# An in-place block solve in two half-groups, work moved between three engines, and adjacent parts for the feed-forward input

## The reference, cut to what matters

```
def _rwkv7_step(S, inp):
    r, w, k, v, a, b = inp
    sa = jnp.einsum('bhvk,bhk->bhv', S, a)
    S = S * w[:, :, None, :] + sa[..., None] * b[:, :, None, :] + v[..., None] * k[:, :, None, :]
    y = jnp.einsum('bhvk,bhk->bhv', S, r)
    return S, y
...
    mean = jnp.mean(y, axis=-1, keepdims=True)
    var = jnp.mean(jnp.square(y - mean), axis=-1, keepdims=True)
    yn = ((y - mean) * lax.rsqrt(var + LNX_EPS)).reshape(B, T, D) * lnx_w + lnx_b
    bonus = (jnp.sum(rh * kh * r_k, axis=-1, keepdims=True) * vh).reshape(B, T, D)
    out = ((yn + bonus) * g).astype(x.dtype)
    return out @ w_o
...
def conv_ffn(x, w_in, conv_w, conv_b, w_out):
    gate, up = jnp.split(x @ w_in, 2, axis=-1)
```

## Time and profile before

| | |
|---|---|
| median of 3 runs | 1096.93 us |
| profiled execution | 1099.76 us, span 1097.9 us |
| TensorE busy | 1071.0 us (98%) |
| VectorE busy | 801.8 us (73%) |
| ScalarE busy | 605.1 us (55%) |
| GpSimd busy | 209.3 us (19%) |
| granted TensorE clock, mean | 0.997 of full speed |
| L288, x960 | 339.8 us busy, 399 ns each |
| L289, x960 | 269.6 us busy, 281 ns each |

### The profile page before, as it was taken

One profiled execution on the slowest core, in us unless ns is written; L12 is line 12 of the kernel. 1 busy time (PEld: TensorE's weight loads), 2 busy tenths in 40 slices (PEclk: granted clock), 3 DMA queues, 4 the chain that ended last, 5 costly groups with the idle time before them and its releaser, 6 DMA issues.

```text
span 1097.9 us, 19100 instructions
## 1 busy us (share of the span) xinstructions
PE 1071.0 (98%) x7335; PEld 924.8 (84%) x7335; DVE 801.8 (73%) x1134; ACT 605.1 (55%) x928; POOL 209.3 (19%) x230
## 2 busy tenths in 40 slices
PE   7999989999999999999999999999999999999997
PEld 6997788888888889789888888998777789888886
DVE  7997887778885758777788746688867776655543
ACT  6765354556664566856566544635665445545532
POOL 0134552112221011001222200470100001122200
PEclk9999999999999999999999999999999999999999
DMA  8553181646666566345667575456452654666552
GB/s 250 170 170 115 46 262 43 172 116 192 185 189 228 196 148 161 118 130 146 188 188 194 174 286 158 155 192 213 148 140 83 194 166 131 184 189 191 192 191 77
DMA packets 219748, 183.13 MB, mean 167 GB/s; under 512 B 43265, under 2 KB 197614, under 8 KB 219678
## 3 DMA queue, kind: packets, MB, share of 16 engines
q1 hardware_dynamic: 215710, 171.43, 52.1%
q0 software_dynamic: 3392, 8.66, 2.5%
q10 hardware_dynamic: 576, 2.07, 0.5%
HBM read 179.44 MB, written 2.69 MB: 166 GB/s over the span
## 4 chain that ended last, share of the span: by engine, by line
PE 82%; DVE 12%; issue 2%; ACT 1%; POOL 1%; DMA 1%; SPq 0%; DVEq 0%; POOLq 0%; ACTq 0%
PE bank L288 21%; PE bank L282 13%; PE bank L284 13%; PE bank L283 13%; PE bank L289 10%; PE bank L295 3%; DVE ring L413 3%; PE bank L1238 2%; DVE arena L1655 1%; DVE arena L1750 1%; DVE stat L1748 1%; PE bank L371 1%; PE bank L2123 1%; PE bank L1353 1%; DVE arena L1680 0%
## 5 line engine op out<-in xcount | busy, mean ns | idle before, releaser
L413 DVE TENSOR_TENSOR ring<-ring,arena 128x2048 fp32r<-128x2048 f32 (+1 forms) x138 | 312.3, 2266 | 113.0 <-ACT arena L407 111.4
L282 PE MATMUL bank<-arena 128*128 128x512 f32 (+3 forms) x980 | 343.8, 351 | 2.0 <-DVE ring L413 1.6
L288 PE MATMUL bank<-arena 128*128 128x512 f32 x960 | 339.8, 399 | 0.0
L407 ACT ACTIVATE arena<-ring 128x2048 fp32r<-128x2048 f32 (+1 forms) x145 | 272.0, 1879 | 93.0 <-DMA ring<-in_ffn_w_out 43.2
L289 PE MATMUL bank<-arena,ring 128*128 128x256 f32 x960 | 269.6, 281 | 0.0
L284 PE MATMUL bank<-arena 128*128 128x512 f32 (+3 forms) x720 | 264.9, 368 | 0.0
L288 PEld LDWEIGHTS bank<-arena 128*128 128x128 f32 x960 | 180.4, 188 | 44.7
L283 PE MATMUL bank<-ring,arena 128*128 128x512 f32 (+2 forms) x560 | 216.2, 386 | 0.0
L282 PEld LDWEIGHTS bank<-arena 128*128 128x128 f32 x980 | 185.5, 189 | 27.1 <-issue 3.7
L289 PEld LDWEIGHTS bank<-arena,ring 128*128 128x128 f32 x960 | 181.5, 189 | 0.0
L284 PEld LDWEIGHTS bank<-arena 128*128 128x128 f32 x720 | 135.6, 188 | 22.3
(11 more groups left out here) (335 smaller groups left out, 1282.7 us busy)
## 6 DMA issues: line engine op xcount, KB each, us to landing
ring<-in_ffn_w_in SPq DMA_DIRECT2D x80, 512.0 KB, 5.1
ring<-in_ffn_w_out SPq DMA_DIRECT2D x44, 512.0 KB, 4.4
ring<-in_w_gate_up SPq DMA_DIRECT2D x40, 512.0 KB, 5.1
ring<-in_w_in SPq DMA_DIRECT2D x18, 1024.0 KB, 5.0
ring<-in_a_w_rkv SPq DMA_DIRECT2D x12, 1024.0 KB, 5.5
ring<-in_w_down SPq DMA_DIRECT2D x22, 512.0 KB, 3.7
ring<-in_a_w_o SPq DMA_DIRECT2D x4, 1024.0 KB, 8.4
arena<-in_ffn_w_in SPq DMA_DIRECT2D x8, 512.0 KB, 4.7
```

The source lines that it names most:

```text
L282: nc.tensor.matmul(dst, stationary[0], moving[0], start=start, stop=False)
L288: nc.tensor.matmul(dst[:, :], stationary[0], both_parts, start=start, stop=False)
L407: nc.scalar.activation(buf(hi_of(n), 0, w, arena12), ring[:, r, 0:w], ACT.Copy).then_inc(hi_ready, 1)
L413: on.tensor_tensor(ring12[:, r, 0:w], ring[:, r, 0:w], buf(hi_of(n), 0, w, arena12).bitcast(F32), ALU.subtract).then_inc(split_ready, 1)
```

## The change

The solve goes by blocks and in place. `block_sweep(a, parts)` computes one block of 32 rows for one half of the heads (g = 0 or 1, 8 heads): 8 matmuls with a stationary operand of 32 columns. Where two parts are given, the two are different row blocks of the two halves, and their matmuls alternate. `block_added` adds those 32 rows (32 x 512) into the right side itself. Half 1 runs one stage behind half 0. `block_inverses` is the old last sweep, one half at a time. `steps` leaves out the first 32 columns. Centring goes from 16 ScalarE instructions a chunk to one on GpSimd, into a buffer of its own; the bonus product goes from VectorE to 16 ScalarE instructions a chunk, and its addition of the shift to GpSimd. SyncE's order changes around w_o, `load_z` and `early_in`. The two parts of the feed-forward input lie next to each other for each chunk of 128 channels, so the 512 columns are one piece.

```diff
-            i, j = sorted((i, j))
-            return arena12[0][:, i:j + 1:j - i, :].rearrange("p s (c t) -> p s c t", t=T)
+            return bufs(i, 2, arena12).rearrange("p (c x t) -> p c x t", x=2, t=T)
...
-        FFN_H, FFN_H_LO, FFN_F, FFN_F_LO, FFN_CONV, FFN_P = (12, 0, 0), (10, 5, 5), 1, 6, 4, 9
+        FFN_H, FFN_F, FFN_F_LO, FFN_CONV, FFN_P = (11, 10, 11), 1, 6, 4, 9
...
-            h2, h_parts = chan2(FFN_H[f], FFN_H_LO[f]), beside(FFN_H[f], FFN_H_LO[f])
+            h2 = parts_of(FFN_H[f])
+            h_parts = bufs(FFN_H[f], 2, arena12).rearrange("p (c n) -> p c n", n=2 * T)
...
-                    mm = nc.tensor.matmul(bank[4 + b % 4][:, i * P:(i + 1) * P], z[a][:, h, :], n_off[a][:, h, :],
+                    mm = nc.tensor.matmul(bank[4 + b % 4][:, i * P + BS:(i + 1) * P], z[a][:, h, :], n_off[a][:, h, BS:P],
...
+            def block_sweep(a, parts):
+                for g, b in parts:
+                    if b > 1:
+                        pe.wait_ge(sum_ready, SUM_NO[a][g, b - 1])
+                    elif a == 0:
                         pe.wait_ge(u_rhs, g + 1)
+                        pe.wait_ge(step_in, 2 * (g + 1))
                     else:
+                        pe.wait_ge(sum_ready, STATE_ADDED + g + 1)
+                        pe.wait_ge(step_in, STEP_BANKS)
+                for i in range(8):
+                    for g, b in parts:
+                        h, cells = 8 * g + i, rows_of_block(b)
+                        mm = nc.tensor.matmul(bank[g][cells, i * N:(i + 1) * N], n_off[a][:, h, cells],
+                                              rhs[a][:, h * N:(h + 1) * N], start=True, stop=True)
+                        if i == 7:
+                            mm.then_inc(sweep_mm, 1)
...
+            def bonus_scaled(a, half):
+                for h in range(8 * half, 8 * half + 8):
+                    op = nc.scalar.activation(bonus[a][:, h // 2, h % 2 * N:(h % 2 + 1) * N], toks(W_V)[:, a, h * N:(h + 1) * N],
+                                              ACT.Copy, scale=bon[:, a * H + h:a * H + h + 1])
...
+            def block_added(a, g, b):
+                rows, cells = rows_of_block(b), slice(g * HALF, (g + 1) * HALF)
+                dve.wait_ge(sweep_mm, SOLVED * a + SWEEP_NO[g, b])
+                nc.vector.tensor_tensor(rhs[a][rows, cells], bank[g][rows, :], rhs[a][rows, cells], ALU.add).then_inc(sum_ready, 1)
...
+            def values_centred(a):
+                pool.wait_ge(means_ready, a + 1)
+                pool.wait_ge(u_mm, 2 * (a + 1))
...
+            def rest_gated(a):
...
+                pool.wait_ge(bonus_copied, NT + a + 1)
+                nc.gpsimd.tensor_tensor(rest[a], bonus[a], chunks(buf(W_LNX, D, 2 * D)), ALU.add).then_inc(c_ready, 1)
+                pool.wait_ge(c_ready, 3 * a + 1)
+                nc.gpsimd.tensor_tensor(rest[a], rest[a], chunks(g), ALU.mult).then_inc(c_ready, 1)
+                pool.wait_ge(c_ready, 3 * a + 2)
                 nc.gpsimd.tensor_tensor(g, g, buf(W_LNX, 0, D), ALU.mult).then_inc(c_ready, 1)
...
+            values_centred(0)
+            values_centred(1)
+            pool.wait_ge(lnx_landed, 32)
+            rest_gated(0)
+            rstd(0)
+            rstd(1)
+            rest_gated(1)
+            rstd(2)
+            rstd(3)
...
+            rows_of("w_o", A["a_w_o"][0], 2, range(0, 1))
             rwkv_inverse_late_sp(sp, 0)
-            rows_of("w_o", A["a_w_o"][0], 2, range(0, 2))
+            rows_of("w_o", A["a_w_o"][0], 2, range(1, 2))
             rwkv_inverse_late_sp(sp, 1)
             rows_of("w_o", A["a_w_o"][0], 2, range(2, 4))
-            sp.wait_ge(sweep_mm, sweeps_before(0, SWEEPS + 1) + 2)
+            sp.wait_ge(ymm, 2)
+            sp.wait_ge(c_ready, 4)
             early_in(0, 0, A["ffn_w_in"][0])
...
-            sp.wait_ge(yn_ready, NT)
-            after_slots(sp, "attn_proj")
+            sp.wait_ge(attn_gated, 4)
             early_in(2, 1, A["w_gate_up_2"][0])
```

More of the change, by code:

```diff
@@ L300, in both, with beside, parts_of @@
             return tuple(v[at] for v in views)
-        def beside(i, j):
-            i, j = sorted((i, j))
-            return arena12[0][:, i:j + 1:j - i, :].rearrange("p s (c t) -> p s c t", t=T)
+        def beside(i):
+            return bufs(i, 2, arena12).rearrange("p (c x t) -> p c x t", x=2, t=T)
+        def parts_of(i):
+            pair = beside(i)
+            return pair[:, :, 0, :], pair[:, :, 1, :]
         def chan2(hi, lo):
@@ L450, in turn_dve @@
         def turn_dve(dve, turn, a, base, hi, lo=None, parts=(0, 1)):
+            hi, lo = (chan(x, arena12) if isinstance(x, int) else x for x in (hi, lo))
             for q in parts:
@@ L688, in ffn_front_dve @@
         def ffn_front_dve(dve, f, i, turn, last):
-            hi, lo, xn = FFN_H[f], FFN_H_LO[f], XN if f else XN_FFN0
+            (hi, lo), xn = parts_of(FFN_H[f]), XN if f else XN_FFN0
             post_scale(dve, i, 0)
@@ L830, in tile @@
                     for k in range(DC):
-                        mm = product_twice(bank[pair + g], both(w, slice(None), k, g), h2[0][:, k], h_parts[:, :, k],
+                        mm = product_twice(bank[pair + g], both(w, slice(None), k, g), h2[0][:, k], h_parts[:, k],
                                            k == 0, k == DC - 1)
@@ L1093, in build @@
                 buf(W_LNX, D, 2 * D).rearrange("p (c t) -> p c t", t=P)]
+        bonus = [rest[0], buf(W_LK[0], D, 2 * D).rearrange("p (c t) -> p c t", t=P)]
         mid, last_e, s_scale = small(16), small(8), small(8)
@@ L1352, in steps @@
                     a, h = b // 4, 4 * (b % 4) + i
-                    mm = nc.tensor.matmul(bank[4 + b % 4][:, i * P:(i + 1) * P], z[a][:, h, :], n_off[a][:, h, :],
+                    mm = nc.tensor.matmul(bank[4 + b % 4][:, i * P + BS:(i + 1) * P], z[a][:, h, :], n_off[a][:, h, BS:P],
                                           start=True, stop=True)
                 mm.then_inc(step_mm, 1)
-            SWEEP_BANK = ((0, 0, 0, 0), (0, 0, 0, 4))
[L1359 to L1363, removed]
-                for g in range(2):
-                    if s == 1 and a == 0:
+            def block_sweep(a, parts):
[3 more added lines that the diff above has]
+                    elif a == 0:
@@ L1379, in y_values, with block_inverses @@
+            def block_inverses(a, g):
+                pe.wait_ge(z_landed, (NT + a + 1) * 16 * NB)
+                pe.wait_ge(sum_ready, SUM_NO[a][g, NB - 1])
+                for i in range(8):
+                    h = 8 * g + i
+                    mm = by_columns(bank[(0, 4)[a] + g][:, i * N:(i + 1) * N], z[a][:, h, :], rhs[a][:, h * N:(h + 1) * N],
+                                    True, True)
+                mm.then_inc(sweep_mm, 1)
             def y_values(a, q):
@@ L1426, in rwkv_pe @@
             y_values(0, 0)
-            y_values(0, 1)
             for h in range(H):
@@ L1448, in rwkv_pe @@
             y_values(1, 0)
+            block_sweep(1, ((0, 2), (1, 1)))
             y_values(1, 1)
-            sweep(1, 1)
             y_state(0)
-            sweep(1, 2)
+            block_sweep(1, ((0, 3), (1, 2)))
             y_state(1)
-            sweep(1, 3)
-            sweep(1, SWEEPS + 1)
+            block_sweep(1, ((1, 3),))
+            block_inverses(1, 0)
             o_turn(0, 0)
-            o_turn(0, 1)
+            block_inverses(1, 1)
             for q in range(2):
```

174 lines of the change are left out of this document (84 added, 90 removed).

## The result

The changed kernel takes 1101.74 us, the median of 20 runs (1097.57 to 1105.35), the kernel before 1095.99 us (20 runs, 1091.87 to 1100.52). The ratio is 1.0043, 95% interval 1.0028 to 1.0058: slower by 4.7 us, clear of noise over 20 runs each though under the 0.5% that three runs could tell, where the prediction said 1086.0 with 1079 to 1094. The profiled execution took 1100.83 us.

A forecast was written before the change was run, and what follows sets the result against it. TensorE was taken as the bound, busy for 1071.0 of 1097.9 us. The terms -6.4, -4.1, -3.0 and +2.6 summed to -10.9 us, giving 1086.0 us, with 1079 to 1094 as the range for 8 in 10.

The forecast's parts named there:

- Feed-forward input, -6.4 us: Feed-forward input: reading 512 columns as one piece saves 6.6 ns on each of 960 pairs, 6.4 us.
- Rival A: Feed-forward input: layout brings nothing, the extra 6.6 ns belong to changing between 512 and 256 columns; 1092.4 us, chance 0.18.
- The sign that the text had set, a period of 0.347: Feed-forward input: a pair period of 0.347 us would show the forecast right, 0.353 rival A.
- TensorE's own work in the solve, -4.1: Solve: 8 sweeps of 16.1 us become block groups and inverses of 12.0 us, -4.1 us.
- rival C: Solve: column groups of 32 don't overlap, +4.0 us, 1090.0 us; chance 0.06.
- The narrower `steps`: Solve: 96 instead of 128 moving columns costed at 0, since the weight load sets the time; -1.9 us if columns counted.
- Idle for instructions, -3.0: Solve: TensorE's idle times without a releaser, read as waits for instructions, lose half of 6.1 us.
- VectorE behind GpSimd, +2.6 (0 to 7.0): Solve and `gated_out(0, 0)`: VectorE instructions wait for GpSimd's doubled 1024-column operations, +2.6 us.
- four exposures, half an operation each on average: Value mean, variance and two `gated_out(0, 0)` operations of VectorE each wait half a GpSimd operation, 4.8 us together.
- a `y_state` of 1.1 us: TensorE has a `y_values` or `y_state` of about 1.1 us to do at two of four exposures, leaving 2.6 us.
- Rival D: VectorE queues behind GpSimd, each of 8 operations holding one instruction for its full length: +8.4 us, 1105.3 us; chance 0.06.
- The sign of being wrong: The prediction is wrong if the pair period doesn't move or the first w_o product starts later than 183.7 us.

The follow-up runs named there:

- the version with all moves: Changed kernel with ScalarE's bonus products and GpSimd's operations earlier, both order moves behind the solve, and value means and first variance reordered: ratio 0.9955, again 0.9968.
- the early bonus: Changed kernel with ScalarE's bonus products moved ahead and GpSimd's `rest_gated(0)` right behind the first centring: 1095.00 us, ratio 0.9999 to the kernel before.
- the solve alone: Kernel before with everything of the change except the feed-forward layout and its weaker wait of `early_in(2, 1)`: 1099.12 us, ratio 1.0052.

## Why the prediction was wrong, point by point

**Feed-forward input, -6.4 us: wrong, 0.** The step that failed is the one that put the 6.6 ns of the earlier trace rows against the earlier trace rows down to the two pieces. The two periods were right, and the cause was not: both periods occur in both layouts, and in the same program from one execution to the next. I read a cost off one execution that happened to have the long state in all three stages, which looked like a constant of the kernel. Rival A had the right end (it wanted 0 for the layout) with another reason: it put the extra down to the change of widths, and both periods have that. The sign that the text had set, a period of 0.347, came in two of the three stages and said nothing of the layout. The layout alone bounds the gain at 0.08% by its interval, 0.9 us. The prediction took from the Trainium skill, "SBUF — State Buffer", the section with the SBUF cachelines, that only leaving a 16-byte line costs, so that two dense pieces cost nothing. The runs agree: 1.0002.

**TensorE's own work in the solve, -4.1: nearly right.** At the same clock 1.00 TensorE is busy for 42.87 us in the kernel before and for 39.82 in the version with all moves, 3.1 less. Two column groups of 32 overlap, 32 records in 1.09 us where 16 of a lone group take 1.08 (rival C falls). The narrower `steps` brought nothing, 3.81 us for 32 records against 3.84 in the earlier trace rows.

**Idle for instructions, -3.0: right in size for the changed kernel.** 4.3 us became 0.87 there, and the solve of the repeated version with all moves has no idle time that ends in "issue"; with the early bonus, 2.36 us came back. I read both idle times as released by neither engine. In one of three profiles of the kernel before the second was VectorE's, behind a held split, and the split there takes 3.85 to 4.47 us in all three and 2.83 in the changed kernel. So a part of the gain can be a shorter hold. Which part, and whether the place of the transfers is the cause of the rest, was not tested.

**VectorE behind GpSimd, +2.6 (0 to 7.0): the mechanism was right, and the size was wrong.** The six operations cost 6.8 us of the changed kernel's solve in its profile and 4.3 by the medians, and the wait of 1.71 us near 141, which the term counted too, comes on top in that profile: about the upper end or beyond it. The step that failed is "four exposures, half an operation each on average". A hold isn't drawn at random: GpSimd's three operations follow each other without a gap, so the first held instruction ends just where GpSimd's next one has begun, and the second then waits for all of that, 2.20 and 2.72 us. I had counted both. Second, I let a `y_state` of 1.1 us cover part of it, but the additions that TensorE needs stood behind both. Third, the granted clock was 0.90 over the solve, with records at about half the pace behind the waits of 1.71 and 4.37 us, which the term didn't have. The length of a wait alone doesn't tell it: behind 1.73 us near 141 in the kernel with the early bonus 32 records took 1.09 us. The Trainium skill, "GPSIMD Engine Reference", section "Specifications", names VectorE instructions with two SBUF inputs or in a two-port mode. The rows agree for the first kind: L1811 and L1813 are held. A scalar step of 8 columns, with one input, is held too; that it ran in a two-port mode no row shows. An addition with a PSUM operand (L1845, 0.69 us at 161.83 beside L1946) and a reduction over SBUF (L1802, 0.68 us at 163.33 beside L1948) are not. Rival D, slower by the same queue, had the mechanism of the result with too low a chance, 0.06.

**What was missing.** The sum had no term for the w_o stage, +3.4 us. The change puts `o_turn(1, 1)` in front of tile (1, 1) instead of (0, 3), and leaves one more split for the time behind the solve, in front of the second chunk's variance; I had costed orders only inside the solve. From the first feed-forward's output products to the second's input products the changed kernel takes 172.0 us (338.40 to 510.40), the one before 170.3; in the other profiles with the new solve it is 170.7 to 171.6, with the old one 170.2 to 170.3. There the sixth of SyncE's eight issues of `kv_w_up` takes 1.85 to 2.72 us in all nine profiles of the new solve, with an instruction transfer of 16 KB inside each, and 0.97 to 1.14 in all five of the old, with no such transfer between 395 and 410 us. It fits a shorter program whose transfers fall elsewhere; no run tested it.

The sum with measured terms, for the changed kernel against the mean of the three profiles of before: solve 50.40 against 48.9 us, +1.5; w_o stage +3.4; +1.7 behind it; together 6.6, where the medians differ by 5.75 and the ratio says 4.7. The stretches come from single profiles, and the solve alone had 47.13 us. The layout doesn't come into it. The sign of being wrong came by a little: the first w_o product after 183.7, at 183.94.

**What stays open.** What picks the long or the short period. What makes the clock fall behind one wait and not behind another of the same length. Whether the layout shifts the odds (4 of 15 against 18 of 27 stages in the profiles) while the times show none of the 2.6 us that this would be.

## What to carry to other kernels

A period read from one execution may be one of two states: profile the same kernel twice before a difference of 2% in a steady loop becomes a term. When work moves to GpSimd, list the VectorE instructions of the kinds that were held here (element by element, all operands in SBUF; a reduction wasn't) that will stand in the queue while it runs, take each wait as full where GpSimd's operations follow each other, and put GpSimd's block where VectorE reads PSUM; moving it a few microseconds later only moved the holds here. Cost the queue orders behind a shortened stage as well, for a gain given back there looks like no gain.

## What the runs showed of the hardware

A steady alternation of a 512- and a 256-column matmul has two stable periods, 346.7 and 353.3 ns, kept for a stage of 320 pairs at a granted clock of 1.00. A VectorE instruction of 8 columns can take 2.37 us, and one of 16 columns 3.90, when GpSimd works on SBUF, and GpSimd's centring 3.96 instead of 1.90 us beside a VectorE split. GpSimd's power on 8 columns (1.65 us) held nothing: L1803 took 0.17 us beside it, at 166.72. TensorE's 4.37 us of idle time were followed by records at half the pace, 16 in 1.92 us. Twelve idle times of TensorE without a releaser ended 1.24 to 1.46 us after an instruction transfer of 16 KB had landed.
